# First shift on VectorE, one buffer for each first piece, and the first attention's pieces moved behind its rotations

## The reference, cut to what matters

```
cs = jax.nn.silu(c)                                  # 1 x 1024
shift, scale, gate = split(cs @ w + b, 3)            # w is 1024 x 3072, one w for each layer
h = x * (1 + scale) + shift                          # in front of the layer
x = layer_norm(ALPHA * x + (1 + gate) * y, g, b)     # behind it
```

## Time and profile before

| | us |
|---|---|
| median of three runs (lowest, highest) | 1787.22 (1781.42, 1788.38) |
| the profiled execution's own time | 1784.72 |
| its span in the profile | 1782.7 |
| PE busy / DVE busy / ACT busy / POOL busy | 1664.5 / 1140.1 / 838.9 / 150.6 |

### The profile page before, as it was taken

How to read it: one execution, slowest core, us unless ns; L and a number is a source line. 1 busy time by engine, 2 the same in 40 slices (tenths; PEclk the granted TensorE clock), 3 DMA queues, 4 the chain that set the end, 5 groups by cost and what they waited for, 6 DMA issues and landing times.

```text
span 1782.7 us, 20551 instructions
## 1 busy us (share of the span) xinstructions
PE 1664.5 (93%) x8247; PEld 1340.6 (75%) x8247; DVE 1140.1 (64%) x1346; ACT 838.9 (47%) x1132; POOL 150.6 (8%) x293
## 2 busy tenths in 40 slices
PE   8777899987889899989999999999999999799998
PEld 3655688865568688878888867888788888578887
DVE  1886867796989856485455887554745556655454
ACT  2443454544234445545344795433643434654443
POOL 3230010005631020000000000000000000000000
PEclk9867999998999899999999989999999999999999
DMA  9658468873019467535655635555545555236552
GB/s 298 239 184 237 165 210 311 305 259 119 1 54 326 164 224 248 182 125 194 218 192 178 210 139 192 186 190 187 191 159 196 189 189 189 95 111 215 181 192 81
DMA packets 165496, 335.45 MB, mean 188 GB/s; under 512 B 38773, under 2 KB 54461, under 8 KB 164250
## 3 DMA queue, kind: packets, MB, share of 16 engines
q1 hardware_dynamic: 144602, 292.63, 48.3%
q0 software_dynamic: 9696, 37.29, 5.8%
q10 hardware_dynamic: 11104, 4.23, 0.9%
HBM read 328.86 MB, written 6.83 MB: 188 GB/s over the span
## 4 chain that ended last, share of the span: by engine, by line
PE 71%; DVE 15%; ACT 5%; issue 3%; POOL 3%; DMA 2%; SPq 1%; DVEq 0%; ACTq 0%; POOLq 0%
PE ps L636 22%; PE ps L638 21%; PE ps L637 21%; DVE wlo L1748 2%; PE ps L721 2%; ACT whi L1204 1%; PE ps L1175 1%; SPq L533 1%; DVE work L2183 1%; DVE xlo L1753 1%; PE ps L715 1%; DMA work<-in_mod_mix_w 1%; POOL mod L2368 1%; POOL mod L2475 1%; DMA raw<-in_mlp_w 1%
## 5 line engine op out<-in xcount | busy, mean ns | idle before, releaser
L1748 DVE TENSOR_TENSOR wlo<-raw,whi 128x2048 fp32r<-128x2048 f32 (+2 forms) x247 | 559.8, 2285 | 269.5 <-ACT whi L1204 269.1
L1204 ACT ACTIVATE whi<-raw 128x2048 fp32r<-128x2048 f32 (+2 forms) x247 | 466.8, 1908 | 227.7 <-PE ps L638 182.8
L636 PE MATMUL ps<-whi,xhi 128*128 128x512 f32 (+2 forms) x1244 | 479.0, 385 | 20.7 <-DVE xlo L1753 20.7
L638 PE MATMUL ps<-whi,xlo 128*128 128x512 f32 (+2 forms) x1244 | 473.4, 381 | 0.0
L637 PE MATMUL ps<-wlo,xhi 128*128 128x512 f32 (+2 forms) x1244 | 473.2, 380 | 0.0
L636 PE MATMUL ps<-whi,hhi 128*128 128x512 f32 x736 | 294.4, 400 | 7.0 <-DVE hlo L1753 6.5
L638 PE MATMUL ps<-whi,hlo 128*128 128x512 f32 x736 | 288.7, 392 | 0.0
L637 PE MATMUL ps<-wlo,hhi 128*128 128x512 f32 x736 | 288.7, 392 | 0.0
L636 PEld LDWEIGHTS ps<-whi,xhi 128*128 128x128 f32 x1244 | 236.5, 190 | 66.5 <-DVE xlo L1753 24.5
L638 PEld LDWEIGHTS ps<-whi,xlo 128*128 128x128 f32 x1244 | 236.3, 190 | 44.5
L637 PEld LDWEIGHTS ps<-wlo,xhi 128*128 128x128 f32 x1244 | 236.6, 190 | 42.1
(11 more groups left out here) (353 smaller groups left out, 1613.0 us busy)
## 6 DMA issues: line engine op xcount, KB each, us to landing
raw<-in_mlp_w SPq DMA_DIRECT2D x64, 1024.0 KB, 5.3
raw<-in_ffn_w_gate SPq DMA_DIRECT2D x44, 1024.0 KB, 5.1
raw<-in_ffn_w_up SPq DMA_DIRECT2D x44, 1024.0 KB, 5.1
raw<-in_ffn_w_down SPq DMA_DIRECT2D x44, 1024.0 KB, 4.9
mod<-in_mod_ffn_w POOLq DMA_DIRECT2D x16, 1024.0 KB, 5.8
mod<-in_mod_mix_w POOLq DMA_DIRECT2D x12, 1024.0 KB, 7.0
work<-in_mod_mix_w SPq DMA_DIRECT2D x8, 1024.0 KB, 8.8
operands<-in_mod_ffn_w SPq DMA_DIRECT2D x8, 1024.0 KB, 7.8
```

What stands on the lines that cost most here:

```text
L636: pe.matmul(o, lh, rh, start=start, stop=False)
L638: return pe.matmul(o, ll, rh, start=False, stop=stop)
L1204: act.activation(whi[:, c % SPL, 0:n], raw[:, c % RAW, 0:n], ACT.Copy).then_inc(hi_done, 1)
L1748: dve.tensor_tensor(wlo[:, c % RAW, 0:n], raw[:, c % RAW, 0:n], whi[:, c % SPL, 0:n].bitcast(F32), ALU.subtract).then_inc(lo_done, 1)
```

## The change

The eight pieces of the first modulation are interleaved (shift, scale, shift, ...), each with its own buffer, so that SP issues them without a wait. DVE sums the four of shift into `GA` (`first_shift`, eight instructions of 1024 columns), and PE spreads that with `ones`; PE sums only the four of scale. On DVE h for the second half of the tokens, now comes behind `x_lo("mla", 0)`. The two bias rows, positions and frequencies are issued by ACT. The thirteen short vectors come as rows of 128 elements into `mod` right behind piece 3, and PE transposes them in one go. The sixteen plus two `s5` input DMAs move from ACT's queue to SP's, behind the norm rows and ahead of chunks 3 and 4. POOL clears `mod` behind `const_ok` and opens the three thirds without waiting between them. `warm_sqrt()` stands ahead of the first norms.

Pieces 4 to 11 use three staging buffers; the third is the pair `GA`, `BA`. In the first attention no piece stands ahead of the rotations. In step i of the loop the piece or `lo` now stands ahead of the rest of head i-3: pieces 0 to 3 at i = 0 to 3, `lo(5)` at 4, piece 4 at 5, `lo(6)` at 6, piece 5 and `lo(7)` at 7, piece 6 at 8 (behind the rest); behind the loop pieces 7, 8, 9, `lo(8)`, pieces 10 and 11. SP loads chunk 9 ahead of pieces 10 and 11, and the two layer norm rows and all later chunks behind piece 9's use. POOL's fetches of 12 to 14 also wait for piece 10's use.

```
-STAGE = [n % 2 if n < 4 else 5 + n % 2 if n < 12 else 2 + (n - 12) % 3 ...]
+STAGE = [n % 2 if n < 4 else 5 + (n - 4) % 3 if n < 12 else 2 + (n - 12) % 3 ...]
 # SP
             for n in range(8):
-                third, kk = n // 4, n % 4
-                if n >= 4:
-                    sp.wait_ge(m0_used, n - 3)
-                sp.dma_start(m0[n % 4], w0[:, 2 * kk:2 * kk + 2, D * third:D * (third + 1)]).then_inc(m0_in[n % 4], 16)
+                third, kk = n % 2, n // 2
+                sp.dma_start(m0[n], w0[:, 2 * kk:2 * kk + 2, D * third:D * (third + 1)]).then_inc(m0_in[n], 16)
+                if n == 3:
+                    for dst, src in vec_rows:
+                        sp.dma_start(dst, src.rearrange("(k p) -> k p", p=P)).then_inc(small2_in, 16)
...
+            sp.wait_ge(mod_clear, 1)
...
+            line(3)
+            line(4)
+            sp.wait_ge(glue_done, 1)
             fetch(sp, 0)
             fetch(sp, 1)
-            for c in range(3, 7):
-                line(c)
-            sp.wait_ge(glue_done, 1)
+            line(5)
+            line(6)
+            fetch(sp, 6)
+            line(7)
+            line(8)
+            sp.wait_ge(pe_pass, passed(4))
+            for n in (4, 5, 2, 3, 7, 8, 9):
+                fetch(sp, n)
+            line(9)
+            fetch(sp, 10)
+            fetch(sp, 11)
+            sp.wait_ge(piece_used, 10)
             load_row("lg1")
             load_row("lb1")
 # PE
+            bias0(1)
+            pe.wait_ge(csb_ok, 1)
+            scale0(0)
+            bias0(0)
...
+            scale0(1)
+            scale0(2)
+            pe.wait_ge(m0_sum, 4)
+            for hf in range(2):
+                pe.matmul(ps[:, hf, :], ones[:, :], GA[:, 512 * hf:512 * (hf + 1)], start=False, stop=True)
+            scale0(3)
 # DVE
+            def first_shift(kks):
+                acc = GA[:, :]
+                for kk in kks:
+                    n = 2 * kk
+                    dve.wait_ge(m0_in[n], 16)
+                    w = m0[n]
+                    if kk == 0:
+                        do(dve.tensor_scalar(acc, w[:, 0, :], csil[:, 0:1], None, ALU.mult))
+                    else:
+                        dve.wait_ge(m0_sum, kk)
+                        do(dve.scalar_tensor_tensor(acc, w[:, 0, :], csil[:, n:n + 1], acc, ALU.mult, ALU.add))
+                    dve.scalar_tensor_tensor(acc, w[:, 1, :], csil[:, n + 1:n + 2], acc, ALU.mult, ALU.add).then_inc(m0_sum, 1)
...
-                piece(0)
                 for g in range(2):
-                    if g:
-                        piece(1)
...
-                lo(5)
                 attention(0)
+                for n in (7, 8, 9):
+                    piece(n)
                 lo(8)
-                piece(10)
-                piece(11)
+                for n in (10, 11):
+                    piece(n)
 # POOL
             for kept in s5_kept:
                 pool.wait_ge(kept, 16)
+            pool.wait_ge(piece_used, 11)
             for n in range(12, 15):
                 fetch(pool, n)
```

More of the change, by code:

```diff
@@ L180 @@
 THIRD_AT = {t: i for i, t in enumerate(THIRDS)}
-STAGE = [n % 2 if n < 4 else 5 + n % 2 if n < 12 else 2 + (n - 12) % 3 for n in range(4 * len(THIRDS))]
+STAGE = [n % 2 if n < 4 else 5 + (n - 4) % 3 if n < 12 else 2 + (n - 12) % 3 for n in range(4 * len(THIRDS))]
 def stage_use(n):
@@ L619, in _ @@
-            for n in range(8, 12):
-                fetch(sp, n)
             for name in phases[1:]:
                 for k in range(dict(PHASES)[name]):
-                    line(FIRST[name] + k)
+                    if FIRST[name] + k > 9:
+                        line(FIRST[name] + k)
                     rows_between(name, k)
@@ L1163, in halves, with bias0, scale0 @@
                 return [ap[:, 512 * q:512 * (q + 1)] for q in range(n)]
+            def bias0(third):
+                for hf, r in enumerate(halves(mod_row[third], 2)):
+                    pe.matmul(ps[:, 2 * third + hf, :], ones[32 * third:32 * third + 1, :], r, start=True, stop=False)
+            def scale0(kk):
+                n = 2 * kk + 1
+                pe.wait_ge(m0_in[n], 16)
+                for hf in range(2):
+                    for k in range(2):
+                        last = pe.matmul(ps[:, 2 + hf, :], csB[:, 2 * kk + k, :], m0[n][:, k, 512 * hf:512 * (hf + 1)],
+                                         start=False, stop=(kk == 3 and k == 1))
+                    if kk == 3:
+                        last.then_inc(m0_done, 1)
@@ new lines, in _ @@
+            scale0(0)
+            bias0(0)
+            pe.wait_ge(s5a_in, 48)
+            pe.wait_ge(s5p_pool, 1)
+            for k in range(3):
+                pe.transpose(ps[:, 7, k * P:k * P + PAIRS], a_rows[:, k, :], ident[0:PAIRS, 0:PAIRS])
+            pe.wait_ge(small2_in, 16 * len(vec_rows))
+            pe.transpose(ps[:, 6, 0:P], vec_stage[:, 0:P], ident[:, :])
+            pe.transpose(ps[:, 6, P:P + 32], vec_stage[0:32, P:2 * P], ident[0:32, 0:32]).then_inc(s5p_ps, 1)
+            scale0(1)
@@ L1433, in mla @@
                 hi(2)
+                warm_sqrt()
                 for tt in range(T):
@@ L1678, in att @@
                 hi(c + 7)
+            for n, r in enumerate(mod_row):
+                act.dma_start(r, mod_b[0][D * n:D * (n + 1)].rearrange("(o n) -> o n", o=1)).then_inc(modb0_in, 16)
+            with nc.allow_non_contiguous_dma(reason="short vectors"):
+                act.dma_start(posi.bitcast(I32), t["positions"][0].rearrange("(t p) -> p t", p=P)).then_inc(pos_in, 16)
+            act.dma_start(invf, t["inv_freq"].rearrange("(o n) -> o n", o=1).to_broadcast([P, 32])).then_inc(pos_in, 16)
             act.wait_ge(c_in, 16)
@@ L2381, in _ @@
                                pattern=[[-1, P]], channel_multiplier=1).then_inc(const_ok, 1)
+            pool.memset(mod[:, 1024:5120], 0.0).then_inc(mod_clear, 1)
             for f in range(3):
-                open_third(f)
+                steps.did(pool.memset(third_tile(f), 0.0))
+            steps.settle()
+            for f in range(3):
+                bias_third(f)
             v = lambda k: g0v[:, k, :]
```

121 lines of the change are left out of this document (53 added, 68 removed).

## The result

The changed kernel takes 1763.39 us (median of 4 runs, 1762.41 to 1764.86) against 1787.80 of the kernel before beside it: a ratio of 0.9871, 95% interval 0.9846 to 0.9896. The profiled execution took 1764.15 with a span of 1762.5. Predicted were 1764.0 us and a range of 1754 to 1775. So sign and size came true. Not all the steps did.

What follows compares the result with a forecast made beforehand. PE's three-part matmuls set the pace over most of the span; the change touches the first 177 us, whose first stage is an order of DMA bytes. -11.1 + 2.0 - 1.3 + 0 - 4.5 - 4.0 - 1.9 = -20.8 us gives 1764, range 1754 to 1775.

Steps and rivals of the forecast that it cites:

- First modulation: First stage: the last piece lands at 30.2 instead of 41.3, -11.1 us, bounds -8.3 and -11.5.
- TensorE's pace behind the landing: Eight records behind the last piece's landing: at PE's slow pace h's second half comes later, +2.0 us, bounds 0 and +3.4.
- The shift's VectorE instructions at 0: First stage: DVE's eight shift instructions cost 0, since the last shift piece lies over 5 us ahead of piece 7.
- Second half of h behind `x_lo`: DVE's first rest no longer waits for h's second half of the tokens: -1.3 us, bounds 0 and -2.8.
- The s5 inputs at 0: s5 input transfers on SP's queue, behind chunks 1, 2 and the norms: 0 us, upper bound +4.9.
- Rotations and gate: Pieces 0 and 1 leave the rotations, which end 6.9 us earlier; with POOL's gate -4.5 us, bounds -3.8 and -6.9.
- the loop has a gate that does not move ... So steps 2 and later gain 3.8 us: Loop start: ACT's L1428 waits for POOL's clearing, so steps 2 and later gain 3.8 us unless POOL is faster.
- The loop: Attention loop: piece ahead of the rest covers the 1.11 us holes; with the loop's end -4.0 us, bounds 0 and -5.8.
- Behind the loop: Last rest to layer norm: five pieces and two `lo`, 17.7 us against 19.6, transfers already there: -1.9 us, bound 0.
- Behind the layer norm nothing is changed ... so the gain stays: After the layer norm: PE sets the pace in unchanged work, so the whole -20.8 us remains to the end.
- does not do what it says: Rival, first stage: shift sum ends last, or slow pieces and PE; gives 5 us instead of 9, 1768 to 1775; chance 0.05.
- Everything is lighter: Rival: POOL ends sooner, PE keeps its pace, 2.0 + 2.4 + 1.5 and 1.5 of the second pass: 1757; chance 0.15.

Runs made afterwards that it cites:

- the second reading: A second profile of the unedited changed kernel, from its second set of 4 runs: 1764.41 us, ratio 0.9878, span 1761.3 us.
- the first reading: The first profile of the unedited changed kernel: profiled execution 1764.15 us, span 1762.5 us; median of its runs 1763.39 us.
- the first stage alone: Changed kernel with attention pieces, staging buffers and the rest of SyncE's order as before the change, only its first stage kept: 1775.42 us, ratio 0.9947.
- the last experiment: Changed kernel with GpSimd's temporaries in the third staging buffer and `wide_row` cleared first, ahead of store and matrices: 1761.20 us, ratio 0.9863.

## Why the prediction was right, and where it was not

**First modulation: right in mechanism, mis-sized in one term.** The step that failed is "The last piece lands at 30.2 instead of 41.3". The bytes were right: the windows up to 30 us sum to 10.1 MB, against 10.35 foreseen by 30.2. But I took the moment when the bytes have been moved for the landing. The landing came 2.6 to 2.9 us later, and the run with nothing behind piece 7 shows that this is the transfer's own tail and not sharing. The prediction quotes the fixed 2.0 us too, and uses only the rate beside it. The term is -8.3 to -8.5, on its bound.

**TensorE's pace behind the landing: +2.0 forecast, +0.9 and 0.0 measured.** The slow pace is a stretch of low granted clock that falls at other places in other profiles of the same kernel. It was in the bounds, but the reason I gave (holes before the last piece) is not borne out: the second reading has a hole and no slow pace. The row it rests on, 0.86 us between records in before, was read wrongly too. That pace has no hole ahead of it; it is the pace of the kernel's start and ends at once (PEld in the timeline of before):

```profile
16.44 0.34 PEld L1175 LDWEIGHTS ps<-work,wide_row 128*128 128x128 f32 x1 [0.52 <-issue]
17.16 0.19 PEld L1175 LDWEIGHTS ps<-work,wide_row 128*128 128x128 f32 x1 [0.39 <-issue]
```

The clock record of that trace begins at 17.0 (in after at 14.4, where the records also go from 0.86 to 0.43), and the 1.00 that the windows give ahead of it is no reading. Twice 0.43 is 0.86, so TensorE started at its lower level (worked out from these rows).

**The shift's VectorE instructions at 0: half right.** The cover I named, "over 5 us", was 33.11 - 27.96 = 5.15 us. The two instructions (2.6) fit in it, but the four records of the spread stand behind them, and at low clock they took until 33.6. So in the first reading the chain came through shift, for 0.5 us. What I did not credit is larger: without this edit the first stage would be 4 to 5 us longer.

**Second half of h behind `x_lo`: right**, -1.4 for -1.3.

**The s5 inputs at 0: right for the wrong weight.** The last issue ended at 49.46, and with 2.0 us to land they were there at 51.5, in time by about 2 us; the run that held chunk 1 shows where this breaks. But their leaving ScalarE's queue is worth 22 to 23 us. The rows of before show these issues at 9.81, 5.68 and 3.87 us, and the prediction did not ask what they would take beside pieces that are all in the queue.

**Rotations and gate: right in size, wrong in its second step.** -5.6 (-5.4) for -4.5; the two halves were -7.5 (-7.3) and +1.9. The step that failed is "the loop has a gate that does not move ... So steps 2 and later gain 3.8 us". The gate moved by 2.4 us more than GpSimd's start (25.3 us from the store to the end of the clearing, 27.7 before), and it holds little: without it head 3 comes 1.1 us sooner and the layer norm 0.5. What gives back is VectorE. From the rotations' end to head 0 it is 1.3 us shorter, since `lo(5)` is gone from there; from head 0 to head 3 it is 3.2 us longer, since piece 0 and a normalizing now run beside GpSimd, 3.0 us slower by their rows. The prediction named contention only as GpSimd's gain and loss, "about nothing in sum", and had no price for VectorE's side of it. That its total came out near is in part luck.

**The loop: right in mechanism, too small.** -6.2 for -4.0, beyond the bound of -5.8. The steps gave 2.7 of the 3.2 us foreseen. The return of 1.5 us for TensorE's slow pace did not occur, and not because the pace was quick; VectorE is busy through it (windows of after):

```profile
122.00:128.00 6.00, 4.96 (x19) 3.98 (x17) 5.83 (x12) 4.45 (x13) 0.00 (x0) 0.50 0.13 52
128.00:134.00 6.00, 3.44 (x9) 2.47 (x10) 5.80 (x9) 0.88 (x3) 0.00 (x0) 0.51 0.88 307
```

The end, from head 7's normalizing to the last rest, gave 3.5 for 2.3. That covering the holes is worth 4.2 to 4.4 us is shown by the run that brings four of them back.

**Behind the loop: right.** -2.1 for -1.9, and the third buffer is worth 3.0 of local waits.

**"Behind the layer norm nothing is changed ... so the gain stays": this failed by 2.4 to 2.5 us.** From one layer norm to the next (second half of the tokens), before took 203.8 and 194.0 us, after 205.1 and 195.7 (the same in the second reading). The work is the same, and so are TensorE's waits in the first of these stretches (6.7 us before, 6.8 after). The windows show the granted clock lower in comparable stretches, here around the end of `mlp0`, first after, then the same stage of before:

```profile
370.00:380.00 10.00, 7.43 (x23) 5.74 (x24) 9.93 (x10) 2.99 (x3) 0.32 (x1) 0.66 0.90 341
```
```profile
390.00:400.00 10.00, 6.35 (x24) 4.85 (x24) 9.83 (x12) 3.99 (x4) 1.05 (x2) 0.83 1.02 390
```

A mean of 0.66 is 3.4 us of work lost in ten, 0.83 is 1.7. The difference of 1.7 us is of the size of the 1.3 missing in `mlp0`. The fourteen profiles fall into two groups. In seven (before, the first stage alone, shift on TensorE, chunk 1 held back, two staging buffers, the s5 inputs on ScalarE, the last experiment) the way from the layer norm to the end takes 1604.9 to 1605.9 us, and their clock records have TensorE at its lower level for 79.5 to 82.7 us of it. In the other seven, both of after among them, it takes 1608.1 to 1608.5, with 86.0 to 89.4 us at the lower level. So these stretches and the missing 2.5 us go together; no run sets them, and which event does stays open. Open too is whether a group belongs to an edit or to one execution: with chunk 1 held back and in the last experiment the profiled execution was the shortest of its four. This is why the third buffer's 3 us look smaller in the total than at the layer norm, and the gate's 0.5 larger.

Of the rivals, the first stage's ("does not do what it says") was nearest: its condition, that shift's sum ends last, came true in one profile, but for 0.5 us instead of 4. Ahead of the layer norm two terms of "Everything is lighter" came true as well: the 2.0 us of TensorE's pace in the second reading, and the loop's 1.5.

Two sums of the prediction are 0.4 us off: its bounds add up to -28.9 and -3.8, not -28.5 and -3.4. Nothing hangs on it.

## What to carry to other kernels

When a transfer is costed by the bytes ahead of it, add the tail of the transfer itself (2.6 to 2.9 us here): bytes moved are not bytes landed. When buffers are added so that one queue never waits, ask what every other queue's issues cost from then on, and which compute instructions stand behind them on that engine; here that side edit was worth as much as the whole change. A gate on the chain is worth only the lead that it has over the next engine: here 0.5 us over VectorE. And read a gain of 3 us at the stage where it arises, since the total moves by as much with TensorE's low clock.

## What the runs showed of the hardware

- One 0.25 MB transfer of short packets held ScalarE's queue for 25.51 us beside an unbroken stream of 4 KB rows, and SyncE's own for 10.35 us behind it.
- The granted clock drops to its lower level (0.50) for some us at places that differ between two executions of one kernel: 30 to 36 us in one, 18 to 24 in the other, with 1.2 us of difference in h, 0.3 of it from the landing.
- In the first 17.0 us of before (14.4 of after) the windows show a granted clock of 1.00 where the trace has no clock record; fp32 records stand 0.86 us apart there and 0.43 behind it.
- An instruction of VectorE with one tensor input took 1.14 us instead of 0.29 beside GpSimd, one with two 1.98 instead of 1.28.
